# GpSimd adds the four squared tiles of a group, TensorE sums one

## The chip, the cores and the metric

One core of a Trainium2 chip runs the whole program in one launch. The metric is the device time in microseconds, the median of several runs.

## What is computed

Three transformer blocks one behind the other on 512 tokens of 1024 numbers, each a mixer and a gated feed-forward layer with norms and residuals around them. The first mixer is a sparse attention, the second a state-space scan (SSD), the third a short convolution. The change lies in the second, in the norm behind the scan:

```python
y = ssd_scan(x_ssm, dt, a, bm, cm) + d_skip[:, None] * x_ssm
y = y.reshape(b, s, 2048) * silu(z)
yg = y.reshape(b, s, 4, 512)
yg = yg * rsqrt(mean(yg * yg, axis=-1) + eps)      # over the 512 channels of a group
y = (yg.reshape(b, s, 2048) * norm_w) @ w_out
```

The scan goes through the tokens in four chunks of 128 and carries a state from one to the next.

## The kernel before

Everything is kept with channels on the 128 partitions and tokens along the free axis. Each engine has a hand-written program; semaphores order them. Large matrix products run as three passes of TensorE (high and low parts of the weights and of the operand), L664 to L666.

The scan consists of 16 steps, G = 4c + g for chunk c and channel group g; the steps of one chunk work on the four groups. What an engine does in a step is written out in a loop on each of them:

- **TensorE**: `segments(G+1)` (L985, two matmuls of 512 columns), `group_sums(G-2)` (L1030), `outputs(G)` (L1008, and from chunk 1 on L1011, which brings in the state), from G+1 = 4 on `spread_cumsums(G+1)` (L991), then `turn_x(G+2)`, `products_cb(G+2)` and, but for the last chunk, `states(G)` (L1021). At two places a `turn_b` stands before `turn_x`.
- **ScalarE**: `segment_exps(G+1)` (L1394), `terms(G+2)` (L1384, eight short ones), `cumsum_exps(G+1)` (L1402, writes xbuf), `keep_b` at two places (L1409), `group_square(G-1)` (L1418, squares of four tiles of 128 tokens into tmp[:, 1, :], 128x512).
- **VectorE**: `weights(G+1)` (L1954, both operands in SBUF), `gated(G)` (L1964, L1968), `x_dt(G+2)` (L1938), `causal_cb(G+2)` (L1945), `keep_state(G)` (L1980, state times decay, from chunk 1 on; L1983 adds the product).
- **GpSimd**: in its loop over n the decayed copy xdec of group n+1 (L599, chunks 0 to 2), then two multiplications of xbuf for group n+1 (L608, chunks 1 to 3), which `outputs(n+1)` waits for.

There is one buffer for the squares: ScalarE writes those of the next group only when TensorE has summed the last ones (`s_gs`). `group_sums` reads the four tiles as weights against a column of ones, so that the sums come out one token to a partition. The sums of the last group, G = 15, run inside the output product behind the scan (`last_sums`); before it stand the norm's steps for the other groups on VectorE and ScalarE and `spread_group` (L1037). A matmul in float32 leaves two records or more in the trace.

Of the kernel before, what the change touches and what calls it, by code (L numbers as in the profile page):

```python
# [9 lines left out]
ALU = mybir.AluOpType  # L10
# [4 lines left out]
P = 128  # L15
S = 512
NT = S // P
# [196 lines left out]
def build(nc, w8, w22, xT, params, heads, w_cmp, w_ada, out):  # L214
    with ExitStack() as ctx:
        def sem(name):
            return ctx.enter_context(nc.semaphore(name))
# [3 lines left out]
        def sb(name, shape, dt=F32, at=None):  # L221
            size = 4 * int(np.prod(shape[1:]))
            size = (size + 31) // 32 * 32
            if at is None:
                at = base[0]
                base[0] += size
            assert at + size <= 229344, (name, at + size)
            t = nc.alloc_sbuf_tensor_at(name, shape, dt, offset=at)
            where[name] = at
            return t  # L230
# [10 lines left out]
        tmp = sb("tmp", [P, 2, S])  # L241
        ident = sb("ident", [P, P])
        ones = sb("ones", [P, P])
# [86 lines left out]
        stat_ps, bc_ps = bank[5], bank[4]  # L330
# [88 lines left out]
        s_cx = sem("c_scaled")  # L419
        s_y = sem("y_made")  # L420
        s_gq = sem("group_squares_made")
        s_gs = sem("group_sums_made")
        s_gn = sem("group_norm_steps")
        s_gr = sem("group_roots_made")
# [47 lines left out]
        def psum_ap(t):  # L472
            return bank[t][:, :]
# [55 lines left out]
        @block.gpsimd  # L529
        def _(pool):  # L530
            chain = Chain(pool, s_pool)
            chain(pool.memset(ident[:, :], 0.0))
            chain(pool.memset(ones[:, :], 1.0))
            chain(pool.memset(mbig[:, :], 0.0))
            chain(pool.memset(mcmp[:, :, :], 0.0))
            chain(pool.memset(rowok[:, :], 1.0))
            chain(pool.memset(pcmp[:, :, :, :, :], 0.0))
            chain(pool.memset(usum[:, :], 1.0))
            chain(pool.memset(after[:, :], 1.0))
            chain.wait()  # L540
            chain(pool.affine_select(out=usum[:, :], in_=usum[:, :], compare_op=ALU.is_ge, fill=0.0,
                                     base=0, pattern=[[1, P]], channel_multiplier=-1))
            chain(pool.affine_select(out=after[:, :], in_=after[:, :], compare_op=ALU.is_ge, fill=0.0,
                                     base=-1, pattern=[[-1, P]], channel_multiplier=1))
            chain(pool.affine_select(out=ident[:, :], in_=ident[:, :], compare_op=ALU.not_equal, fill=1.0,
                                     base=0, pattern=[[-1, P]], channel_multiplier=1))

            chain(pool.affine_select(out=mbig[:, :], in_=mbig[:, :], compare_op=ALU.is_ge, fill=NEG,
                                     base=S - P, pattern=[[-1, S]], channel_multiplier=1))

            chain(pool.affine_select(out=mcmp[:, :, :], in_=mcmp[:, :, :], compare_op=ALU.is_ge, fill=NEG,
                                     base=-31, pattern=[[P, NT], [-16, NC]], channel_multiplier=1))
            chain(pool.affine_select(out=rowok[:, :], in_=rowok[:, :], compare_op=ALU.is_ge, fill=0.0,
                                     base=-31, pattern=[[0, 1]], channel_multiplier=1))
            chain.wait()
            pool.memset(small[:, 31:32], 0.0).then_inc(s_const, 1)

            def add_update(before):

                for j in range(KD):  # L560
                    pool.wait_ge(s_add, before + j + 1)
                    pool.tensor_tensor(h[:, j, :], tmp[:, j % 2, :], h[:, j, :], ALU.add).then_inc(s_h, 1)  # L562

            def ada(half):

                for s in range(ADA_HALF * half, ADA_HALF * (half + 1)):
                    acc = ada_acc[:, s % 2, :]
                    for k in range(KD):
                        n = KD * s + k
                        w = ada_w[:, n % ADA_RING, :]  # L570
                        pool.wait_ge(s_ada_w[n % ADA_RING], 16 * (n // ADA_RING + 1))
                        if k == 0:
                            if s >= 2:
                                pool.wait_ge(s_adap, s - 1)
                            pool.tensor_scalar(acc, w, csil[:, 0:1], 1.0, ALU.mult, ALU.mult).then_inc(s_ada_k, 1)  # L575
                            continue
                        chain(pool.tensor_scalar(w, w, csil[:, k:k + 1], 1.0, ALU.mult, ALU.mult))  # L577
                        chain.wait()
                        pool.wait_ge(s_ada_k, n)
                        pool.tensor_tensor(acc, acc, w, ALU.add).then_inc(s_ada_k, 1)  # L580

            pool.wait_ge(s_sq, 1)
            pool.memset(vz[:, :, :, :], 0.0).then_inc(s_vz, 1)
            pool.wait_ge(s_csil, 1)
            add_update(0)
            ada(0)
            add_update(KD)
            for n in range(-1, 4 * NT):
                c, g = (n + 1) // 4, (n + 1) % 4
                if c >= NT:  # L590
                    continue
                if c < NT - 1:

                    pool.wait_ge(s_xd, n + 2)
                    pool.wait_ge(s_dec, 1)
                    if c:
                        pool.wait_ge(s_st, n - 2)
                    hs = slice(8 * g, 8 * g + 8)
                    pool.tensor_tensor(xdec[:, hs, :], xdt[:, hs, :],  # L599
                                       acs[:, 1, c, hs].unsqueeze(2).to_broadcast([P, 8, HD]),  # L600
                                       ALU.mult).then_inc(s_xdec, 1)
                if c:
                    tok = slice(c * P, (c + 1) * P)
                    for U in (2 * n + 2, 2 * n + 3):

                        pool.wait_ge(s_xe, U - 8 + 1)
                        b = xbuf[:, U % 4, :].rearrange("p (a l) -> p a l", a=4)
                        pool.tensor_tensor(b, b, cv[:, 4 + g, tok].unsqueeze(1).to_broadcast([P, 4, P]),  # L608
                                           ALU.mult).then_inc(s_cx, 1)
            add_update(2 * KD)  # L610
            ada(1)

# [2 lines left out]
        def _(pe):  # L615
# [44 lines left out]
            def product(bk, g, kb, k, last, hi, lo):  # L660

                w = g % SLOTS
                cols = slice(kb * P, (kb + 1) * P)
                pe.matmul(bk, whi[w][:, cols], hi[:, k, :], start=k == 0, stop=False)  # L664
                pe.matmul(bk, whi[w][:, cols], lo[:, k, :], start=False, stop=False)  # L665
                return pe.matmul(bk, wlo[w][:, cols], hi[:, k, :], start=False, stop=last)  # L666
# [62 lines left out]
            for kb in range(KD):  # L729
                pe.wait_ge(s_xt, XT["NSA_IN"] + kb + 1)  # L730
                for c in range(3):
                    if kb == 0:
                        pe.wait_ge(s_lo, c + 1)
                    mm = product(psum_ap(c), c, kb, kb, kb == KD - 1, xhi, xlo)
# [16 lines left out]
            for c in range(V_FIRST, V_FIRST + 4):  # L751
                pe.wait_ge(s_lo, c + 1)
                w = c % SLOTS
                for kk in range(2):
                    k = 2 * (c - V_FIRST) + kk
                    cols = slice(kk * S, (kk + 1) * S)
                    for t in range(NT):
# [4 lines left out]
                        mm = pe.matmul(bk, xlo[:, k, tk], whi[w][:, cols], start=False, stop=k == KD - 1)  # L762
# [26 lines left out]
            for g in range(4):  # L789
                for hh in range(2):  # L790
                    mm = pe.matmul(bank[4][(g % 2) * HD:(g % 2 + 1) * HD, (g // 2) * NC:(g // 2 + 1) * NC],
                                   w2[0][:, hh, :], hg[:, hh, g, 0:NC], start=hh == 0, stop=hh == 1)
# [5 lines left out]
            for g in range(4):  # L798
                for hh in range(2):
                    mm = pe.matmul(bank[5][:, g * HD:(g + 1) * HD],  # L800
                                   hv[:, hh, g, :, :].rearrange("p q c -> p (q c)"),
                                   w2[1][:, hh, :], start=hh == 0, stop=hh == 1)
            mm.then_inc(s_cm, 1)
            pe.wait_ge(s_gate, 1)
            for t in range(NT):
                mm = pe.transpose(bank[6][:, t * 48:(t + 1) * 48], gt[:, t * P:(t + 1) * P], ident[0:48, 0:48])
# [218 lines left out]
            def group_sums(G):  # L1025

                c, g = G // 4, G % 4
                pe.wait_ge(s_gq, G + 1)
                for r in range(4):
                    mm = pe.matmul(stat_ps[:, 4 * g + c:4 * g + c + 1], tmp[:, 1, r * P:(r + 1) * P], ones[:, 0:1],  # L1030
                                   start=r == 0, stop=r == 3)
                mm.then_inc(s_gs, 1)

            def spread_group(g):

# [14 lines left out]
            for G in range(4 * NT):  # L1050
                c, g = G // 4, G % 4
# [14 lines left out]
                if c < NT - 1:  # L1066
                    states(G)
            group_sums(4 * NT - 2)

            pe.wait_ge(s_gn, 2)  # L1070
# [7 lines left out]
            def last_sums():  # L1078

                group_sums(4 * NT - 1)  # L1080
# [1139 lines left out]
```

## Time and profile before

| | |
|---|---|
| median of three runs | 2267.5 us (2264.09 to 2268.2) |
| the profiled execution, its own time | 2270.14 us |
| its span, first to last instruction | 2268.4 us |
| TensorE busy | 2174.0 us (96%) |
| VectorE, ScalarE, GpSimd busy | 1269.9, 854.4, 289.4 us |
| mean granted clock of TensorE | 0.971 of 2.4 GHz |

Busy time is the sum of an engine's instructions, the span what passes from the first to the last; an engine's share says only how much of the time it works, not whether others wait for it. The scan lies between about 1030 and 1152 us of the span.

### The profile page before, as it was taken

Reading aid. Unit: us, or ns where it says so; the run is one execution under the profiler, and the core shown is the slowest. Engines: PE = TensorE matmul, PEld = TensorE weight load, DVE = VectorE, ACT = ScalarE, POOL = GpSimd, SP = SyncE. Lnnn points to the kernel's source line nnn. Section 1 sums busy time; section 2 is a strip of 40 time slices with the busy share of each in tenths; the row PEclk is TensorE's granted clock in tenths of the full one; section 3 lists DMA queues with packets and bytes.
Section 4 is the critical chain, followed back from the end, with each engine's and each line's share of the span. In section 5 each row is a group of like instructions: output and inputs, shape, how many; then the busy total and the mean of one; then the engine's idle time right before and its main releaser. Section 6 shows DMA issues by size and latency. Waiting matters only on the chain.

```text
span 2268.4 us, 27014 instructions
## 1 busy us (share of the span) xinstructions
PE 2174.0 (96%) x10560; PEld 1728.7 (76%) x10560; DVE 1269.9 (56%) x2112; ACT 854.4 (38%) x1438; POOL 289.4 (13%) x200
## 2 busy tenths in 40 slices
PE   8999989999999999998999999999999999999997
PEld 6876667788888778885678788888778877888885
DVE  4267663777755578636763687764455445333333
ACT  4156662444432254426642444432221223222221
POOL 0000000200029600002400200009700000000000
PEclk9999989999999999999999999999979988999998
DMA  8210002233246423220013132236512212223231
GB/s 260 61 41 29 20 11 65 65 103 95 96 135 199 145 75 111 93 91 22 1 29 102 51 117 93 93 114 197 181 49 91 93 65 75 93 95 98 89 93 54
DMA packets 59790, 203.57 MB, mean 90 GB/s; under 512 B 6800, under 2 KB 7312, under 8 KB 59408
## 3 DMA queue, kind: packets, MB, share of 16 engines
q1 hardware_dynamic: 55920, 191.36, 26.2%
q10 hardware_dynamic: 3744, 10.49, 1.4%
q8 instruction: 84, 1.38, 0.2%
q14 instruction: 42, 0.34, 0.0%
HBM read 197.63 MB, written 2.10 MB: 88 GB/s over the span
## 4 chain that ended last, share of the span: by engine, by line
PE 90%; DVE 5%; ACT 4%; issue 1%; POOL 1%; DMA 0%; SPq 0%; DVEq 0%; ACTq 0%; POOLq 0%
PE bank L664 25%; PE bank L665 25%; PE bank L666 25%; PE bank L619 2%; ACT pbuf L1268 1%; PE bank L985 1%; PE bank L774 1%; PE bank L869 1%; DVE pbuf L1740 1%; PE bank L991 1%; PE bank L823 1%; PE bank L846 1%; PE bank L646 1%; PE bank L1008 1%; ACT pt L1285 1%
## 5 line engine op out<-in xcount | busy, mean ns | idle before, releaser
L664 PE MATMUL bank<-xhi,whi 128*128 128x512 f32 x1712 | 686.6, 401 | 28.9 <-DVE xlo L1515 22.6
L665 PE MATMUL bank<-xlo,whi 128*128 128x512 f32 x1712 | 681.1, 398 | 0.0
L666 PE MATMUL bank<-xhi,wlo 128*128 128x512 f32 x1712 | 680.9, 398 | 0.0
L1125 ACT ACTIVATE whi<-raw 128x1024 fp32r<-128x1024 f32 (+1 forms) x322 | 334.2, 1040 | 773.3 <-PE bank L666 706.1
L1503 DVE TENSOR_TENSOR wlo<-raw,whi 128x1024 fp32r<-128x1024 f32 (+1 forms) x322 | 412.4, 1282 | 367.9 <-ACT whi L1125 367.2
L664 PEld LDWEIGHTS bank<-xhi,whi 128*128 128x128 f32 x1712 | 324.5, 190 | 110.5 <-issue 13.1
L666 PEld LDWEIGHTS bank<-xhi,wlo 128*128 128x128 f32 x1712 | 323.9, 189 | 79.6
L665 PEld LDWEIGHTS bank<-xlo,whi 128*128 128x128 f32 x1712 | 324.6, 190 | 77.1
L664 PE MATMUL bank<-hid_hi,whi 128*128 128x512 f32 x528 | 209.5, 397 | 0.0
L665 PE MATMUL bank<-hid_lo,whi 128*128 128x512 f32 x528 | 208.6, 395 | 0.0
L666 PE MATMUL bank<-hid_hi,wlo 128*128 128x512 f32 x528 | 208.5, 395 | 0.0
L666 PEld LDWEIGHTS bank<-hid_hi,wlo 128*128 128x128 f32 x528 | 99.0, 187 | 24.2
L665 PEld LDWEIGHTS bank<-hid_lo,whi 128*128 128x128 f32 x528 | 99.0, 188 | 23.8
L664 PEld LDWEIGHTS bank<-hid_hi,whi 128*128 128x128 f32 x528 | 99.0, 188 | 23.7
L580 POOL TENSOR_TENSOR ada_acc<-ada_acc,ada_w 128x768 f32<-128x768 f32 x56 | 116.0, 2071 | 4.7
L1619 DVE TENSOR_TENSOR upad<-bank,rstd_b 128x512 f32<-128x512 f32 x88 | 60.6, 690 | 78.0 <-PE bank L666 71.6
L562 POOL TENSOR_TENSOR h<-tmp,h 128x512 f32<-128x512 f32 x24 | 38.0, 1619 | 497.4 <-DVE tmp L1546 497.4
L1183 ACT ACTIVATE tmp<-upad,par 128x512 f32<-128x512 f32 x88 | 70.6, 804 | 27.0 <-DVE upad L1619 27.0
L1268 ACT ACTIVATE pbuf<-pbuf,stat 128x512 f32<-128x512 f32 (+3 forms) x128 | 70.1, 551 | 23.7 <-DVE stat L1743 23.7
L575 POOL TENSOR_SCALAR ada_acc<-ada_w,csil 128x768 f32<-128x768 f32 x8 | 12.2, 1524 | 509.4 <-DMA ada_w<-w_ada 509.4
L577 POOL TENSOR_SCALAR ada_w<-ada_w,csil 128x768 f32<-128x768 f32 x56 | 74.8, 1335 | 0.8 <-DMA ada_w<-w_ada 0.7
L1631 DVE SCALAR_TENSOR_TENSOR tmp<-upad,par,tmp 128x512 f32<-128x512 f32 x88 | 66.2, 752 | 3.1
(271 smaller groups left out, 2540.7 us busy)
## 6 DMA issues: line engine op xcount, KB each, us to landing
raw<-w SPq DMA_DIRECT2D x298, 512.0 KB, 3.6
ada_w<-w_ada SPq DMA_DIRECT2D x64, 384.0 KB, 3.1
raw<-w SPq DMA_DIRECT2D x24, 384.0 KB, 3.4
h<-xT ACTq DMA_DIRECT2D x8, 256.0 KB, 9.4
w_k<-w_cmp ACTq DMA_DIRECT2D x1, 2048.0 KB, 8.5
w_v<-w_cmp ACTq DMA_DIRECT2D x1, 2048.0 KB, 7.8
out_t<-h ACTq DMA_DIRECT2D x8, 256.0 KB, 2.0
dk<-stg ACTq DMA_DIRECT2D x2, 256.0 KB, 6.8
```

The lines of the kernel that those rows point to most:

```text
L577: chain(pool.tensor_scalar(w, w, csil[:, k:k + 1], 1.0, ALU.mult, ALU.mult))
L580: pool.tensor_tensor(acc, acc, w, ALU.add).then_inc(s_ada_k, 1)
L619: mm = pe.matmul(stat_ps[:, t:t + 1], src[:, t * P:(t + 1) * P], ones[:, 0:1], start=first and t == 0, stop=last, skip_group_check=True)
L664: pe.matmul(bk, whi[w][:, cols], hi[:, k, :], start=k == 0, stop=False)
L665: pe.matmul(bk, whi[w][:, cols], lo[:, k, :], start=False, stop=False)
L666: return pe.matmul(bk, wlo[w][:, cols], hi[:, k, :], start=False, stop=last)
L1125: act.activation(whi[g % SLOTS][:, 0:n], raw[g % RAWS][:, 0:n], ACT.Copy).then_inc(s_hi, 1)
L1183: act.activation(tmp[:, c % 2, :], upad[:, c % 2, 2:2 + S], ACT.Identity, scale=col("ffn_w", 3 * k + 2), bias=col("ffn_b", k)).then_inc(s_ ...
L1268: act.activation(pbuf[:, s % 3, g, 0:n], pbuf[:, s % 3, g, 0:n], ACT.Exp, scale=QSCALE, bias=stat[:, b, 4 + g:5 + g], accum_out=stat[:, b, ...
L1503: dve.tensor_tensor(wlo[g % SLOTS][:, 0:n], raw[g % RAWS][:, 0:n], whi[g % SLOTS][:, 0:n].bitcast(F32), ALU.subtract).then_inc(s_lo, 1)
L1619: dve.tensor_tensor(upad[:, c % 2, 2:2 + S], in_bank(c)[:, :], rstd_b[:, :], ALU.mult)\
L1631: ins = dve.scalar_tensor_tensor(out=tmp[:, v, :], in0=upad[:, v, 0:S], scalar=col("ffn_w", 3 * k), in1=tmp[:, v, :], op0=ALU.mult, op1=AL ...
```

## The change

GpSimd gets `add_squares(G)`: it waits for the squares of group G, adds tiles 2 and 3 onto tiles 0 and 1 (128x256), waits for its own result, and adds tile 1 onto tile 0 (128x128). Then it signals `s_ga`. It does so in its loop for group n-1, behind the work for group n+1; the last two groups stand behind the loop. TensorE waits for `s_ga` in the place of `s_gq` and makes one matmul on tile 0 in the place of four. Nothing else is changed; ScalarE's squares still wait for TensorE's sums.

```diff
+        s_ga = sem("group_squares_added")
...
+            def add_squares(G):
+
+                pool.wait_ge(s_gq, G + 1)
+                chain(pool.tensor_tensor(tmp[:, 1, 0:2 * P], tmp[:, 1, 0:2 * P], tmp[:, 1, 2 * P:4 * P], ALU.add))
+                chain.wait()
+                pool.tensor_tensor(tmp[:, 1, 0:P], tmp[:, 1, 0:P], tmp[:, 1, P:2 * P], ALU.add).then_inc(s_ga, 1)
+
             for n in range(-1, 4 * NT):
                 c, g = (n + 1) // 4, (n + 1) % 4
                 if c >= NT:
...
                         pool.tensor_tensor(b, b, cv[:, 4 + g, tok].unsqueeze(1).to_broadcast([P, 4, P]),
                                            ALU.mult).then_inc(s_cx, 1)
+                if n >= 1:
+                    add_squares(n - 1)
+            for G in (4 * NT - 2, 4 * NT - 1):
+                add_squares(G)
             add_update(2 * KD)
...
             def group_sums(G):
 
                 c, g = G // 4, G % 4
-                pe.wait_ge(s_gq, G + 1)
-                for r in range(4):
-                    mm = pe.matmul(stat_ps[:, 4 * g + c:4 * g + c + 1], tmp[:, 1, r * P:(r + 1) * P], ones[:, 0:1],
-                                   start=r == 0, stop=r == 3)
-                mm.then_inc(s_gs, 1)
+                pe.wait_ge(s_ga, G + 1)
+                pe.matmul(stat_ps[:, 4 * g + c:4 * g + c + 1], tmp[:, 1, 0:P], ones[:, 0:1],
+                          start=True, stop=True).then_inc(s_gs, 1)
```

The line numbers of the changed kernel are 8 higher in GpSimd's loop and 12 higher on TensorE. GpSimd's order in chunk 2, before (xdec, xbuf: the multiplications named above; the words in brackets are the semaphores waited for):

```order
L608 TENSOR_TENSOR xbuf<-xbuf,cv 128x512 [waits spread_exps] x2
L599 TENSOR_TENSOR xdec<-xdt,acs 128x512 [waits state_products,decays_made,x_dt_made]
L608 TENSOR_TENSOR xbuf<-xbuf,cv 128x512 [waits spread_exps] x2
L599 TENSOR_TENSOR xdec<-xdt,acs 128x512 [waits state_products,decays_made,x_dt_made]
L608 TENSOR_TENSOR xbuf<-xbuf,cv 128x512 [waits spread_exps] x2
```

and in the changed kernel:

```order
L616 TENSOR_TENSOR xbuf<-xbuf,cv 128x512 [waits spread_exps] x2
L592 TENSOR_TENSOR tmp<-tmp 128x256 [waits group_squares_made]
L594 TENSOR_TENSOR tmp<-tmp 128x128 [waits pool_chain]
L607 TENSOR_TENSOR xdec<-xdt,acs 128x512 [waits state_products,decays_made,x_dt_made]
L616 TENSOR_TENSOR xbuf<-xbuf,cv 128x512 [waits spread_exps] x2
L592 TENSOR_TENSOR tmp<-tmp 128x256 [waits group_squares_made]
L594 TENSOR_TENSOR tmp<-tmp 128x128 [waits pool_chain]
```

The two additions of group n-1 stand directly behind the two xbuf multiplications of group n+1 and ahead of the next xdec.

TensorE's order around the same place, before (the banks and buffers with their numbers; L985 is segments, L1030 the sums, L1008 and L1011 the outputs):

```order
L985 MATMUL bank0<-vbuf2_124,after_121 128x512 [waits spread_exps,segment_terms_made]
L985 MATMUL bank1<-vbuf3_125,after_121 128x512 [waits spread_exps,segment_terms_made]
L1030 MATMUL bank5<-ones_66,tmp_64 128x1 [waits group_squares_made]
L1030 MATMUL bank5<-ones_66,tmp_64 128x1 x3
L1008 MATMUL bank2<-ebuf_119,xdt_114 64x128 [waits c_scaled,ssd_weights_made,state_kept,y_kept,x_dt_made]
```

and in the changed kernel:

```order
L997 MATMUL bank0<-vbuf2_124,after_121 128x512 [waits spread_exps,segment_terms_made]
L997 MATMUL bank1<-vbuf3_125,after_121 128x512 [waits spread_exps,segment_terms_made]
L1041 MATMUL bank5<-ones_66,tmp_64 128x1 [waits group_squares_added]
L1020 MATMUL bank2<-ebuf_119,xdt_114 64x128 [waits c_scaled,ssd_weights_made,state_kept,y_kept,x_dt_made]
```

Three matmuls are gone; the one left stands at the same place, in front of the outputs, and waits for GpSimd in the place of ScalarE.

## Rows read from the trace of the kernel before

**Rows 1.** The page, part 4: shares of the chain that ended last.
```profile
PE 90%; DVE 5%; ACT 4%; issue 1%; POOL 1%; DMA 0%; SPq 0%; DVEq 0%; ACTq 0%; POOLq 0%
```

**Rows 2.** Timeline of step 9: start us, us, engine, line, operation, [idle before <-releaser].
```profile
1090.34 1.98 PE L991 MATMUL bank<-vbuf,ones 128*128 128x512 f32 x4
...
1092.17 2.50 POOL L608 TENSOR_TENSOR xbuf<-xbuf,cv 128x512 f32<-128x512 f32 x2 [5.45 <-ACT xbuf L1402]
...
1092.85 0.62 ACT L1418 ACTIVATE tmp<-zb 128x512 f32<-128x512 f32 x1
...
1093.88 1.34 DVE L1980 TENSOR_TENSOR state<-state,acs 128x512 f32<-128x512 f32 x1 [0.20 <-PE bank L1021]
...
1094.62 1.50 POOL L599 TENSOR_TENSOR xdec<-xdt,acs 128x512 f32<-128x512 f32 x1
...
1095.39 0.95 PE L1030 MATMUL bank<-ones,tmp 128*128 128x1 f32 x8
...
1095.86 1.41 DVE L1954 TENSOR_TENSOR sqr<-sqr,cbuf 128x512 f32<-128x512 f32 x2
...
1096.27 0.45 PE L1008 MATMUL bank<-ebuf,xdt 128*64 128x128 f32 x4
...
1098.22 1.98 PE L991 MATMUL bank<-vbuf,ones 128*128 128x512 f32 x4
```

**Rows 3.** Timeline of step 13, in the last chunk.
```profile
1129.76 1.98 PE L991 MATMUL bank<-vbuf,ones 128*128 128x512 f32 x4
...
1131.60 2.50 POOL L608 TENSOR_TENSOR xbuf<-xbuf,cv 128x512 f32<-128x512 f32 x2 [5.39 <-ACT xbuf L1402]
...
1133.96 0.95 PE L1030 MATMUL bank<-ones,tmp 128*128 128x1 f32 x8
...
1134.00 1.48 DVE L1954 TENSOR_TENSOR ebuf<-ebuf,cbuf 128x512 f32<-128x512 f32 x2 [0.90 <-ACT ebuf L1394]
...
1134.84 0.45 PE L1008 MATMUL bank<-sqr,xdt 128*64 128x128 f32 x4
```

**Rows 4.** Timeline of step 15.
```profile
1143.81 1.98 PE L991 MATMUL bank<-vbuf,ones 128*128 128x512 f32 x4
...
1147.00 1.05 PE L1030 MATMUL bank<-ones,tmp 128*128 128x1 f32 x8 [1.20 <-ACT tmp L1418]
...
1147.98 0.45 PE L1008 MATMUL bank<-sqr,xdt 128*64 128x128 f32 x4
```

**Rows 5.** GpSimd by line: duration ns min/median/max; the last row: busy us, mean ns, idle us before.
```profile
L562 POOL TENSOR_TENSOR h<-tmp,h x24: 1260/1732/1762, 399.3 to 1269.4; 128x512 f32<-128x512 f32 x24
...
L580 POOL TENSOR_TENSOR ada_acc<-ada_acc,ada_w x56: 1817/1854/2702, 668.6 to 1626.6; 128x768 f32<-128x768 f32 x56
...
L599 POOL TENSOR_TENSOR xdec<-xdt,acs x12: 1041/1249/1497, 1037.1 to 1110.4; 128x512 f32<-128x512 f32 x12
...
L580 POOL TENSOR_TENSOR ada_acc<-ada_acc,ada_w 128x768 f32<-128x768 f32 x56 | 116.0, 2071 | 4.7
```

**Rows 6.** Timeline of step 1: VectorE and GpSimd together.
```profile
1039.78 2.14 DVE L1954 TENSOR_TENSOR sqr<-sqr,cbuf 128x512 f32<-128x512 f32 x2
...
1039.93 1.45 POOL L599 TENSOR_TENSOR xdec<-xdt,acs 128x512 f32<-128x512 f32 x1 [1.83 <-DVE xdt L1938]
```

**Rows 7.** Timeline of steps 3 and 7: two places where ScalarE is last.
```profile
1058.57 0.60 ACT L1402 ACTIVATE xbuf<-bank 128x512 f32<-128x512 f32 x1
...
1084.22 0.66 PE L964 MATMUL bank<-ident,cv 128*128 128x128 f32 x4 [0.74 <-ACT btok L1409]
```

**Rows 8.** Waits of TensorE (timeline), and windows: length, busy, granted clock, DMA.
```profile
219.31 1.14 PE L846 MATMUL bank<-ident,pbuf 128*128 128x128 f32 x8 [1.43 <-ACT pt L1285]
...
1165.44 0.50 PE L664 MATMUL bank<-yhi,whi 128*128 128x512 f32 x1 [1.51 <-DVE ylo L2006]
...
1148.00:1150.00 2.00, 2.00 (x34) 1.00 0.00 0
1166.00:1170.00 4.00, 4.00 (x12) 0.57 0.00 0
```


## The prediction

> **What bounds the kernel now.** I read four views: the page's chain of work that ended last, the timeline of one step of the scan, the rows of GpSimd's groups, and the granted clock around TensorE's long waits. The chain says that 90% of the span ends on TensorE [rows 1]. So a TensorE instruction less is worth its time, as long as nothing else becomes the last to arrive. In the scan that has to be looked at step by step.
>
> Take the step G = 9 (chunk 2) [rows 2]. I count from t0, the start of spread_cumsums(9) on TensorE at 1090.34. ScalarE takes the exponential of the first bank, and GpSimd starts scaling xbuf at t0+1.83; its two multiplications take 2.50 us, and its next instruction starts at 1094.62, t0+4.28. Meanwhile ScalarE made the squares of group 7 at 1092.85, well before. TensorE, without a gap, does segments(10), then the sums of group 7 at 1095.39, then outputs(9) at 1096.27, t0+5.93, and spread_cumsums(10) at 1098.22: a period of 7.88 us with no wait of TensorE. The eight records of the sums (two passes for each of four matmuls) hold it from 1095.39 to 1096.27, 0.88 us, 0.11 us each.
>
> In the last chunk a step is shorter, because it has no state product: from t0 = 1129.76 to outputs(13) at 1134.84 is 5.08 us, though GpSimd's two multiplications stand at the same distance from t0 [rows 3]. In the last step, outputs(15) follows t0 = 1143.81 by 4.17 us, after a wait of 1.20 us for the squares [rows 4].
>
> **What the change removes.** Three of four matmuls per group: 6 of 8 records, 6/8 of 0.88 = 0.66 us, and for 16 groups 10.6 us at most.
>
> **What it adds.** On GpSimd two additions a group, 128x256 and 128x128, both from SBUF to SBUF, 32 instructions. The trace has no such shape. Nearest are the two-input instructions of 128x512 (1260 ns at the least) and 128x768 (1817 ns at the least) [rows 5]: 557 ns for 256 columns, 2.18 ns a column, and some 145 ns apart from the columns. That gives 0.70 and 0.42 us. The second waits for the first by a semaphore: behind such a wait the 56 accumulations of 128x768 sat idle 4.7 us in all, 0.08 us each. The pair takes **1.20 us** undisturbed. From below: the fastest 128x512 row, 1041 ns with a broadcast operand, taken by its columns alone, gives 0.78 us for 384 columns. From above: each addition once held up by a VectorE instruction, which comes next. The Trainium skill, "GPSIMD Engine Reference", section 3.1, measures 4497 ns for an addition of 2048 columns; an estimate in proportion is 0.84 us for the pair, and the sum below would be some 3 us smaller by it. The same section says that VectorE should do elementwise work, which speaks against this change.
>
> **VectorE holds GpSimd up.** A VectorE instruction with two operands in SBUF and a GpSimd instruction exclude each other in this trace. VectorE's weights, of the same shape, take some 0.7 us each; its state <- state,acs starts at 1093.88, lasts 1.34, and so ends 1095.22, while GpSimd's multiplication was running until about 1094.6; GpSimd's xdec, started at 1094.62, then takes 1.50 instead of 1.04 us [rows 2, 5]. So xdec really began at t0+4.74. A second case shows who comes next: VectorE started a pair at 1039.78 and GpSimd one at 1039.93, which ended at 1041.38; the pair took 2.14 us instead of some 1.4 [rows 6]. GpSimd got in between the two, 0.56 us behind the start of the first (1041.38 - 1.04 - 1039.78). The Trainium skill, "SBUF — State Buffer", section "Who interferes with whom", has it as a rule: whoever gets the shared ports first keeps them for the whole instruction. By that rule, the trace agrees, additions placed where xdec stands now are held up as xdec is.
>
> **Where the additions stand.** In GpSimd's order add_squares(G-2) comes right behind the two multiplications of group G, so it cannot start before t0+4.28, although its squares are ready at t0+3.1. TensorE must have it for the sums, and outputs(G) is queued behind the sums; behind that, spread_cumsums(G+1), which starts the next period. So the loop spread, exponential, two multiplications, two additions, sums, outputs, spread becomes a closed one through four engines.
>
> - **Steps 5 to 12** (VectorE's state update runs there). First addition 4.74 + 0.70 = 5.44; second from 5.52. VectorE's weights start at 1095.86, also t0+5.52: a tie. If GpSimd wins, it ends at 5.94; if VectorE wins, GpSimd gets in at about 6.08 and ends at 6.50. Add 0.05 us for the semaphore and 0.32 us for the two records of a drained TensorE (the last but one sums took 0.98 us from 1147.00 to 1147.98 for eight; less 0.66) [rows 4]. outputs(G) starts at 6.31 or 6.87 instead of 5.93: +0.38 or +0.94; I take the middle, +0.66. In step 7 TensorE waits for ScalarE's copy of B anyway, so that its period is longer [rows 7], the additions are covered, and the 0.66 us is won. Seven steps: +4.6 (2.7 to 6.6); one: -0.7.
> - **Steps 13 and 14.** VectorE's weights are first in line at t0+4.24 (1134.00) and, having waited for GpSimd's multiplication, start about 0.1 later; GpSimd follows 0.56 behind, at 4.90, and ends the first addition at 5.60. The second half of the weights then takes 0.69 from about 5.5, GpSimd gets in at 6.1 and ends at 6.5; outputs start at 6.9 instead of 5.08. +1.8 each, **+3.6**. Undisturbed it would be 4.28 + 1.20 + 0.37 = 5.85, +0.77.
> - **Step 15.** No weights follow; outputs(15) at t0+5.85 instead of 4.17: **+1.7**.
> - **Steps 2 to 4**: nothing. In step 4 the multiplications wait for ScalarE, which at 1058.57 comes to the exponential without an idle moment [rows 7], so an earlier spread wins nothing.
> - **Last sums**, inside the next matrix product: four matmuls become one, **-0.7**; the addition was done long before.
>
> Together 4.6 - 0.7 + 3.6 + 1.7 - 0.7 = **+8.5 us**.
>
> **The clock.** TensorE's new waits: in steps 13 and 14 from where the sums stand now (1133.96, t0+4.2) to 6.5, 2.3 us; in step 15 from t0+1.98 to 5.5, 3.5 us; in steps 5 to 12 from 5.05 to 5.95 or 6.5, 0.9 to 1.4 us. Of the eight waits of 1.4 to 2.9 us that TensorE has between 200 us and the product behind the scan, six were followed by a fall to 1.2 GHz (the first is that of 1.43 us, the last that of 1.51 us); behind the one of 1.20 us the clock stayed at 1.00 [rows 4, 8]. Behind the last, the clock stood at 0.57 over 4 us: 0.43 of 4 us, 1.7 us lost. Three new long waits, six in eight, 1.7 us: **+3.8**.
>
> **Sum.** +12.3 us on the profiled execution's 2270.1: 2282.4. That execution lies 2.6 above the median of the runs, 2267.5, so the forecast for a median is **2280**.
>
> **Rivals.**
> 1. *The additions are not held up* (0.20). For it: xdec takes 1.04 us at the least and 1.25 in the middle of its twelve rows, so about half were not held up, and the two sides could fall clear of each other once the period shifts. Against: at this very place it was, by 0.46 us [rows 2, 5]. Then outputs start at 5.85: seven steps -0.1 each, step 7 -0.7, steps 13 and 14 +0.8 each, 15 +1.7, last sums -0.7: +1.2, with one fall of the clock +2.9: **2270.5**, inside the noise.
> 2. *Faster: TensorE's saving comes through* (0.06). For it: TensorE bounds the scan, and GpSimd idles 5.4 us before the xbuf multiplications shown [rows 2, 3]. It needs the additions ready where the sums stand now, t0+5.05, that is a pair of at most 0.7 us (5.05 - 4.28 - 0.05) that nothing holds up; the lower bound is 0.78 us. Then steps 5 to 12 and the last sums win 0.66 us each, -5.9; steps 13 and 14 have outputs at 4.28 + 0.7 + 0.37 = 5.35, +0.3 each, and step 15 +1.2: -4.1, **2263**. At a pair of 1.3 us (5.93 - 0.37 - 4.28) nothing is left of the gain in steps 5 to 12.
> 3. *The clock falls in steps 5 to 12 too* (0.12). The waits there, 0.9 to 1.4 us, recur every 8 us. Eight more falls at 1.7 us: +14, **2294**.
>
> The forecast case (held up, clock falling in the last chunk) has 0.62.
>
> **How the numbers follow.** Its own range is 2275 (GpSimd wins every tie, one fall) to 2284 (VectorE wins, three falls). The range takes in rival 1 and most of the way to rival 3: **2269 to 2291**. Differences below 0.2%, 4.5 us, can't be told from no change. Slower than 2272: 0.62, 0.12 and 0.02 of rival 1, less 0.01 where the ties all go one way, 0.75. Faster than 2263: most of rival 2 and what may be missing from both views, 0.05. Within: 0.20.
>
> **What the changed profile would show.** Right: TensorE's sums shrink to 32 records; in front of them a new idle row with GpSimd's second addition as the releaser, 0.7 us or more in steps 5 to 12 and about 2 in 13 and 14; the 128x256 additions at 0.70 us alone and above 1.1 beside VectorE; periods of 8.3 to 8.8 us in chunks 1 and 2 and about 9 in chunk 3; a granted clock below 1.00 between 1130 and 1155. Wrong: additions of 0.5 us, periods of 7.2 us and no idle row; or a clock of 0.5 all through chunks 1 and 2.

## The result, and the profile after

| | before | changed |
|---|---|---|
| median of four runs | 2267.85 us | 2283.03 us |
| lowest to highest | 2264.09 to 2270.28 | 2279.79 to 2285.03 |
| the profiled execution's span | 2268.4 us | 2278.0 us |

The ratio is 1.0067, with an interval of 1.0048 to 1.0086: the changed kernel is slower by 15 us. A second measurement on another occasion gave 2282.5 us and a ratio of 1.0073 (1.0061 to 1.0086). The profiled execution was the fastest of its four, so its span shows less than the medians.

The page of the changed kernel: TensorE has 96 records less and 10 us less of busy time, GpSimd 27 us more; in the chain that ended last (second row) TensorE's share fell from 90% to 87% and GpSimd's rose from 1% to 3% [rows 1]. The freed engine now waits in the chain for the one that got the work.

```profile
PE 2163.6 (95%) x10464; PEld 1715.8 (75%) x10464; DVE 1270.3 (56%) x2112; ACT 854.5 (38%) x1438; POOL 316.1 (14%) x232
...
PE 87%; DVE 5%; ACT 4%; POOL 3%; issue 1%; DMA 0%; SPq 0%; DVEq 0%; POOLq 0%; ACTq 0%
```

One label first. TensorE's first spread is that of group 4, at 1057.40 before the change; counted from there, the spread at 1090.34 is the fifth, that of group 8. So the step of [rows 2], which the prediction calls step 9, is step 8, with the sums of group 6. Its times and sums are not touched by this: steps 8 to 12 all have the same period. (The rows under experiments 1, 3, 4 and 6 are of step 9 itself.) A step G is here what passes from spread_cumsums(G) to the next spread.

The timeline of step 8, which answers to [rows 2] (L1003 is the spread, L616 the multiplications, L1428 the squares, L1990 the state update, L592 and L594 the additions, L1964 the weights, L1041 the sums, L1020 the outputs):

```profile
1089.09 1.98 PE L1003 MATMUL bank<-vbuf,ones 128*128 128x512 f32 x4
...
1090.92 2.49 POOL L616 TENSOR_TENSOR xbuf<-xbuf,cv 128x512 f32<-128x512 f32 x2 [3.50 <-ACT xbuf L1412]
...
1091.60 0.62 ACT L1428 ACTIVATE tmp<-zb 128x512 f32<-128x512 f32 x1
...
1092.63 1.33 DVE L1990 TENSOR_TENSOR state<-state,acs 128x512 f32<-128x512 f32 x1 [0.20 <-PE bank L1033]
...
1093.37 1.17 POOL L592 TENSOR_TENSOR tmp<-tmp 128x256 f32<-128x256 f32 x1
...
1094.60 1.54 DVE L1964 TENSOR_TENSOR sqr<-sqr,cbuf 128x512 f32<-128x512 f32 x2
1094.62 0.97 POOL L594 TENSOR_TENSOR tmp<-tmp 128x128 f32<-128x128 f32 x1
...
1095.65 0.38 PE L1041 MATMUL bank<-ones,tmp 128*128 128x1 f32 x2 [1.34 <-POOL tmp L594]
...
1095.96 0.45 PE L1020 MATMUL bank<-ebuf,xdt 128*64 128x128 f32 x4
...
1097.91 1.98 PE L1003 MATMUL bank<-vbuf,ones 128*128 128x512 f32 x4
```

With t0 = 1089.09 everything up to 1093.37 lies where it lay before: GpSimd's next instruction starts at t0+4.28, which is now the first addition. It takes 1.17 us: VectorE's state update, issued at t0+3.54, ran first when the multiplication ended (experiment 6 takes it away). VectorE's weights and the second addition start almost together, at t0+5.51 and t0+5.53, and the addition takes 0.97 us. TensorE has waited 1.34 us when the sums may start, and outputs(8) begins at t0+6.87 in place of t0+5.93. The next spread is at t0+8.82, not 7.88.

The next rows are the starts of the spread and of the sums on TensorE, in brackets its wait and who ended it, in steps 4 and 5 and from step 13 to the norm behind the scan:

```profile
1054.00 1.98 PE L1003 MATMUL bank<-vbuf,ones 128*128 128x512 f32 x4
...
1060.55 0.38 PE L1041 MATMUL bank<-ones,tmp 128*128 128x1 f32 x2 [1.33 <-POOL tmp L594]
...
1062.81 1.98 PE L1003 MATMUL bank<-vbuf,ones 128*128 128x512 f32 x4
...
1080.48 1.98 PE L1003 MATMUL bank<-vbuf,ones 128*128 128x512 f32 x4
...
1133.23 1.98 PE L1003 MATMUL bank<-vbuf,ones 128*128 128x512 f32 x4
...
1139.66 0.38 PE L1041 MATMUL bank<-ones,tmp 128*128 128x1 f32 x2 [2.07 <-POOL tmp L594]
...
1141.92 1.98 PE L1003 MATMUL bank<-vbuf,ones 128*128 128x512 f32 x4
...
1148.36 0.38 PE L1041 MATMUL bank<-ones,tmp 128*128 128x1 f32 x2 [2.07 <-POOL tmp L594]
...
1151.98 2.22 PE L1003 MATMUL bank<-vbuf,ones 128*128 128x512 f32 x4
1157.80 0.38 PE L1041 MATMUL bank<-ones,tmp 128*128 128x1 f32 x2 [3.60 <-POOL tmp L594]
...
1163.75 5.49 PE L1047 MATMUL bank<-ident,gst 128*128 128x128 f32 x24 [2.45 <-DVE gst L2028]
```

| stretch | before, us | changed, us | difference |
|---|---|---|---|
| step 4, spread to spread | 7.89 | 8.81 | +0.9 |
| steps 5, 6 and 8 to 12, each | 7.88 | 8.83 | +0.95, seven times +6.6 |
| step 7 | 9.28 | 8.61 | -0.7 |
| step 13 | 7.03 | 8.69 | +1.7 |
| step 14 | 7.02 | 10.06 | +3.0 |
| step 15 to the norm (L1037, now L1047) | 9.16 | 11.77 | +2.6 |

That is +14.2 us from the spread of step 4 to the norm. In the profile of the second measurement the same stretch is longer by 2.2 us: 16.4 above the kernel before. Ahead of it, from the scan's first segments (1031.58 before, 1029.34 now) to that spread, 25.8 became 24.7 us; behind it, from the norm to the end, 1115.4 became 1114.3 us.

Step 13 answers to [rows 3]. VectorE's weights were first, the addition got in between their two halves, and the second addition behind the second half:

```profile
1137.47 1.82 DVE L1964 TENSOR_TENSOR ebuf<-ebuf,cbuf 128x512 f32<-128x512 f32 x2 [0.90 <-ACT ebuf L1404]
1137.53 1.22 POOL L592 TENSOR_TENSOR tmp<-tmp 128x256 f32<-128x256 f32 x1
...
1138.83 0.78 POOL L594 TENSOR_TENSOR tmp<-tmp 128x128 f32<-128x128 f32 x1
```

The two kinds of addition over all 16 groups (minimum, median and maximum in ns, of 128x256 and of 128x128):

```profile
L592 POOL TENSOR_TENSOR tmp<-tmp x16: 716/1173/1222, 1045.1 to 1163.4; 128x256 f32<-128x256 f32 x16
```

```profile
L594 POOL TENSOR_TENSOR tmp<-tmp x16: 452/820/975, 1046.2 to 1164.2; 128x128 f32<-128x128 f32 x16
```

And TensorE's clock in the last chunk (length, busy time, granted clock, DMA):

```profile
1130.00:1140.00 10.00, 6.96 (x52) 1.00 0.00 0
1140.00:1148.00 8.00, 6.29 (x47) 1.00 0.01 2
1148.00:1150.00 2.00, 1.64 (x18) 0.77 0.00 0
1150.00:1152.00 2.00, 2.00 (x21) 0.50 0.00 0
1152.00:1154.00 2.00, 2.00 (x5) 0.88 0.00 0
1159.00:1161.00 2.00, 2.00 (x23) 0.58 0.00 0
```

It answers to [rows 8]: 1.00 through the waits of steps 12 and 13 (and in all of 1046 to 1130), then 0.50 behind the 2.07 us wait of step 14, and 0.58 behind the 3.60 us of step 15.

### The profile page after: what moved, and what is told of

Its sections match the earlier page's. It is cut to its first block, busy times and chain, and to the rows that moved or that the text cites. A ratio compares the mean times of both kernels' runs of the same rounds, so it can differ in the third digit from the quotient of the medians.

```text
span 2278.0 us, 26854 instructions
## 1 busy us (share of the span) xinstructions
PE 2163.6 (95%) x10464; PEld 1715.8 (75%) x10464; DVE 1270.3 (56%) x2112; ACT 854.5 (38%) x1438; POOL 316.1 (14%) x232
## 3 DMA queue, kind: packets, MB, share of 16 engines
q8 instruction: 83, 1.36, 0.2%
## 4 chain that ended last, share of the span: by engine, by line
PE 87%; DVE 5%; ACT 4%; POOL 3%; issue 1%; DMA 0%; SPq 0%; DVEq 0%; POOLq 0%; ACTq 0%
PE bank L676 25%; PE bank L677 25%; PE bank L678 25%; PE bank L631 2%; ACT pbuf L1278 2%; DVE pbuf L1750 1%; PE bank L786 1%; POOL xbuf L616 1%; PE bank L881 1%; PE bank L835 1%; PE bank L858 1%; PE bank L658 1%; PE bank L1020 1%; POOL h L563 1%; ACT pt L1295 1%
```

## The experiments

All were timed against the kernel before on the same chip. t0 is always the start of the spread.

**1. The sums one place later.**

```diff
-                if G >= 2:
-                    if G == 2:
-                        pe.wait_ge(s_acv, 1)
-                    group_sums(G - 2)
                 outputs(G)
+                if G >= 2:
+                    if G == 2:
+                        pe.wait_ge(s_acv, 1)
+                    group_sums(G - 2)
```

> The changed kernel with one thing moved: on TensorE the sums of group G-2 stand behind outputs(G) in place of in front of it. Nothing is left out. If the cost is the closed loop (multiplications, additions, sums, outputs, spread), the additions, ready some 6.5 us after t0, are covered by the outputs, which then end about 7.2 us after t0; every wait of 1.3 to 3.6 us before the sums goes, the steps win 0.66 us each, and the time is about 2260 us, 7 us under the kernel before. If the cost is GpSimd's additions themselves, by holding up VectorE wherever the sums stand, it stays near 2283 us.

Measured: 2261.73 us, ratio 0.9971 (0.9959 to 0.9982). The additions are the same, the 15 us are gone, and 6 us of gain stand in their place (7 were expected). A second measurement, for its timeline:

> The kernel with the sums behind the outputs, once more, for its timeline: 2259 to 2263 us. By the closed loop outputs(9) starts 5.2 to 5.3 us after t0, GpSimd's additions still take 1.2 and 1.0 us beside VectorE, and no wait stands before the sums but in step 15.

Measured: 2261.05 us, ratio 0.9973 (0.9964 to 0.9983).

```profile
1096.78 1.96 PE L1003 MATMUL bank<-vbuf,ones 128*128 128x512 f32 x4
...
1098.60 2.50 POOL L616 TENSOR_TENSOR xbuf<-xbuf,cv 128x512 f32<-128x512 f32 x2 [1.19 <-ACT xbuf L1412]
...
1101.05 1.18 POOL L592 TENSOR_TENSOR tmp<-tmp 128x256 f32<-128x256 f32 x1
...
1101.91 0.45 PE L1020 MATMUL bank<-sqr,xdt 128*64 128x128 f32 x4
...
1102.31 0.97 POOL L594 TENSOR_TENSOR tmp<-tmp 128x128 f32<-128x128 f32 x1
...
1103.86 0.38 PE L1041 MATMUL bank<-ones,tmp 128*128 128x1 f32 x2
...
1104.10 1.96 PE L1003 MATMUL bank<-vbuf,ones 128*128 128x512 f32 x4
```

The second addition still ends at t0+6.5, but outputs(G) no longer waits for it: it starts at t0+5.13, and the sums find their tile ready, with no idle time in brackets. The period is 7.32 us, 0.56 less than in the kernel before. No wait stands before the sums of any step. What is left is in step 15: 1.38 us before the outputs, for GpSimd's multiplication, and behind them 2.62 us before the last but one sums, on which only the norm waits.

**2. The same move in the kernel before.**

> The kernel before with the same move: its four matmuls of group G-2 stand behind outputs(G). Nothing is left out. It tells whether the move alone is worth something. The kernel before waits for the sums only in step 15, and there the path ends on the norm's first step, which comes out at the same time by either order; so both theories expect 2266 to 2269 us, no change.

Measured: 2268.13 us, ratio 1.0005 (0.9996 to 1.0014). The move by itself wins nothing. So experiment 1's gain is the change's own saving, which the closed loop had hidden.

**3. The signal without the additions.**

```diff
-                chain(pool.tensor_tensor(tmp[:, 1, 0:2 * P], tmp[:, 1, 0:2 * P], tmp[:, 1, 2 * P:4 * P], ALU.add))
-                chain.wait()
-                pool.tensor_tensor(tmp[:, 1, 0:P], tmp[:, 1, 0:P], tmp[:, 1, P:2 * P], ALU.add).then_inc(s_ga, 1)
+                pool.memset(small[:, 24:25], 0.0).then_inc(s_ga, 1)
```

> The changed kernel without the additions: GpSimd clears one column of a small tile at their place and signals. It leaves out the adding, so that TensorE sums only the first of the four squared tiles. The queue order and all waits stay. If the length of the additions is what costs, the signal comes 4.4 us after t0, outputs start at 4.8 to 5.3, and the time is about 2261 us. If the place behind the two multiplications, or the signal through a fourth engine, is enough, steps 5 to 12 still wait and the time stays above 2270 us.

Measured: 2261.06 us, ratio 0.9968 (0.9956 to 0.9980).

```profile
1094.96 1.98 PE L1001 MATMUL bank<-vbuf,ones 128*128 128x512 f32 x4
...
1099.23 0.10 POOL L592 MEMSET small<- 128x1 f32 x1
...
1100.02 0.28 PE L1039 MATMUL bank<-ones,tmp 128*128 128x1 f32 x2
...
1102.17 1.98 PE L1001 MATMUL bank<-vbuf,ones 128*128 128x512 f32 x4
```

The signal comes at t0+4.4, the sums start at t0+5.06 behind the segments with no wait, the period is 7.21 us. The place in GpSimd's queue and the handover through it cost nothing in chunks 1 and 2, nor in steps 13 and 14, which show no wait before the sums either; the length of the additions does. In step 15 alone the place has a price: TensorE waits 2.43 us for the signal there, where the kernel before waited 1.20 us for the squares.

**4. One addition.**

```diff
-                chain(pool.tensor_tensor(tmp[:, 1, 0:2 * P], ...))
-                chain.wait()
-                pool.tensor_tensor(tmp[:, 1, 0:P], ...).then_inc(s_ga, 1)
+                pool.tensor_tensor(tmp[:, 1, 0:2 * P], tmp[:, 1, 0:2 * P], tmp[:, 1, 2 * P:4 * P],
+                                   ALU.add).then_inc(s_ga, 1)
...
-                pe.matmul(... tmp[:, 1, 0:P] ...)
+                for r in range(2):
+                    mm = pe.matmul(... tmp[:, 1, r * P:(r + 1) * P] ..., start=r == 0, stop=r == 1)
```

> The changed kernel with the first addition alone (128x256); TensorE sums two tiles in place of one. Nothing is left out. By the closed loop outputs start 5.45 + 0.05 + 0.54 = 6.04 us after t0, 0.1 later than before in steps 5 to 12, 1.0 in steps 13 and 14, 1.4 in step 15, less 0.44 in step 7 and in the last sums: +3.3 us, with one fall of the clock +5: 2271 to 2273 us. If the cost went by the count of groups, whatever the additions take, it would be near the 2283 us of the changed kernel.

Measured: 2272.07 us, ratio 1.0019 (1.0010 to 1.0028).

```profile
1101.35 1.18 POOL L592 TENSOR_TENSOR tmp<-tmp 128x256 f32<-128x256 f32 x1
...
1102.58 0.61 PE L1041 MATMUL bank<-ones,tmp 128*128 128x1 f32 x4 [0.30 <-POOL tmp L592]
```

The addition ends at 1102.53, and TensorE waits 0.30 us in place of 1.34. The period is 8.00 us (the sums start at 1102.58 and again at 1110.58), 0.12 above the kernel before. So half the work on each side comes out nearly even in chunks 1 and 2, as the sum of the loop's parts says.

**5. Additions for the first eleven groups alone.** In the sums `if G > 10` takes the old wait and the four matmuls, and GpSimd's loop adds for `1 <= n <= 11` only.

> The changed kernel, with GpSimd's additions for groups 0 to 10 alone; the sums of groups 11 to 15 (steps 13 to 15, the last but one and those in the output product) are four matmuls behind ScalarE's squares, as before. Nothing is left out. By the closed loop and its clock what is left is steps 5 to 12: +0.94 in seven, -0.66 in step 7, about +5.9 us: 2273 to 2274 us, with no fall of the clock in chunk 3. If the last three steps cost nothing of their own, it stays at 2283 us; if the waits in steps 5 to 12 are covered, it falls to 2267 us.

Measured: 2274.16 us, ratio 1.0040 (1.0027 to 1.0054), beside 2282.5 for the changed kernel. Some 7 us belong to steps 4 to 12, some 8 to steps 13 to 15 and what follows. In its timeline TensorE waits 1.34 to 1.36 us before the sums of steps 8 to 12, as in the changed kernel, and 1.21 us in step 15, as before the change.

**6. The instruction that holds the first addition up.**

```diff
-                    chain(dve.tensor_tensor(state[:, hs, :], state[:, hs, :],
-                                            acs[:, 2, c, hs].unsqueeze(2).to_broadcast([P, 8, HD]), ALU.mult))
-                    chain.wait()
                     dve.tensor_tensor(state[:, hs, :], state[:, hs, :], pr, ALU.add).then_inc(s_stk, 1)
```

> The changed kernel without VectorE's product of the state with its decay (the state is summed undecayed, so the outputs differ). It takes away the instruction that holds up the first addition. By the ports the first addition takes 0.72 us in steps 5 to 12 in place of 1.17 and ends at t0+5.0; the second meets VectorE's weights in a tie, so that outputs start at 5.9 to 6.4 in place of 6.87: 3 to 7 us off the changed kernel, 2276 to 2280 us. If the additions are long of themselves, they stay at 1.17 and 0.97 us, and the time at 2283 us.

Measured: 2279.11 us, ratio 1.0053 (1.0040 to 1.0066); its runs (2275.03 to 2280.57) lie wholly under those of the changed kernel beside it (2281.23 to 2283.82).

```profile
1095.04 1.98 PE L1003 MATMUL bank<-vbuf,ones 128*128 128x512 f32 x4
...
1099.33 0.74 POOL L592 TENSOR_TENSOR tmp<-tmp 128x256 f32<-128x256 f32 x1
...
1100.14 1.55 DVE L1964 TENSOR_TENSOR ebuf<-ebuf,cbuf 128x512 f32<-128x512 f32 x2 [0.87 <-ACT ebuf L1404]
1100.14 1.00 POOL L594 TENSOR_TENSOR tmp<-tmp 128x128 f32<-128x128 f32 x1
...
1101.51 0.45 PE L1020 MATMUL bank<-sqr,xdt 128*64 128x128 f32 x4
...
1103.46 1.98 PE L1003 MATMUL bank<-vbuf,ones 128*128 128x512 f32 x4
```

The first addition starts at t0+4.29 as ever and takes 0.74 us in place of 1.17. The second, now 0.4 us earlier, starts in the same hundredth as VectorE's weights (L1964), which were earlier too, and takes 1.00 us. outputs(G) starts at t0+6.47 in place of 6.87, the period is 8.42 us: the outputs come a little later than the 6.4 us that I had expected at most. Seven steps shorter by 0.41 us are 2.9 us, and the medians differ by 3.4.

**7. The waits filled.**

```diff
+                    if G >= 13:
+                        for r in range(3 if G < 15 else 6):
+                            pe.matmul(bank[5][:, 256:384], ones[:, :], ident[:, :], start=True, stop=True)
                     group_sums(G - 2)
```

> The changed kernel with spare matmuls of 128 columns in front of the sums of steps 13, 14 (three each, 1.3 us) and 15 (six, 2.6 us), into unused columns. Nothing is left out. They lie in waits of 2.1 and 3.6 us and lengthen nothing. If the clock's falls in the last chunk are part of the cost, it stays at 1.00 from 1130 to 1160 us, outputs take 1.95 us in each step, and the time is 2 to 4 us under the changed kernel. If the falls cost nothing, the times are equal.

> The changed kernel itself, beside the other three on the same chip: 2280 to 2285 us.

Measured: 2278.95 us (2278.72 to 2280.67), ratio 1.0059 (1.0046 to 1.0072), against 2282.5 us (2281.23 to 2283.82), ratio 1.0073. The intervals of the ratios overlap, the runs do not, and the mean granted clock was 0.972 in all five runs with filled waits, 0.969 in all five of the changed kernel. The same stretch of both, first the kernel with filled waits, then the changed kernel, with the 4 us behind its waits of steps 13 and 14:

```profile
1134.00:1160.00 26.00, 20.81 (x162) 0.99 0.00 1
```

```profile
1134.00:1160.00 26.00, 18.26 (x104) 0.87 0.00 1
1140.00:1144.00 4.00, 4.00 (x35) 0.59 0.01 4
1150.00:1154.00 4.00, 3.87 (x35) 0.57 0.00 0
```

In this execution of the changed kernel both waits of 2.07 us were followed by half the clock; in the one shown above only the second was, and so it was in the profile of experiment 6. The spare matmuls keep the clock at 0.99 up to step 15, and TensorE's remaining wait before the sums there is 1.40 us in steps 13 and 14. They did not keep the clock up in step 15, where 2.27 us of waiting were left and the clock was 0.67 from 1160 to 1164.

**8. One place later still.** The sums stand behind `spread_cumsums(G + 1)`.

> The changed kernel with the sums behind spread_cumsums(G+1), one place later still, so that nothing of the loop is queued behind them. Nothing is left out. If the sums behind the outputs are covered already, it is the same, 2260 to 2263 us. If they hold up the spread there, even by their own 0.22 us a step, it is some 2 us faster.

Measured: 2260.46 us, ratio 0.9972 (0.9963 to 0.9982). Its period is 7.27 us (1099.56 to 1106.83), 0.05 under that of experiment 1; the times cannot be told apart. Both beat the kernel before by 0.3%, and the changed kernel by 1%.

## Why the prediction was right

**The direction and its cause.** The forecast was that the additions enter a loop through four engines, in front of the outputs. Experiments 1 and 3 show both halves: the same additions off the loop cost nothing, and the loop without their length costs nothing but a longer wait in step 15. GpSimd's work as such, and its hold on VectorE, is no cost here: in experiment 1 it is all there.

**Steps 5 to 12.** I took the middle of a tie at t0+5.52, +0.66; VectorE went first in every step, and outputs start at 6.87, the very upper value. Seven steps cost 6.6 us in place of 4.6. Undisturbed, the additions took 0.72 and 0.45 us; I had 0.70 and 0.42, from the slope between two longer rows. Experiment 6 shows the reason of the rest for the first addition: without VectorE's state update it takes 0.74 us in place of 1.17. For the second, no run takes the weights away; its 0.97 us beside them, against 0.45 in step 15, where no weights run, is the evidence. Step 7 won 0.7 us as computed.

**Steps 2 to 4.** Here a step failed: "nothing". Step 4 costs 0.9 us. I had only asked whether an earlier spread would help, and not placed the additions: VectorE does not yet multiply the state by its decay there, so the first takes 0.72 us, but the second (0.79 us) has to take turns with the weights, whose pair takes 1.95 us, and outputs(4) starts at t0+6.87. It is the same loop. What saved part of the sum is that the stretch ahead of step 4 is 1.2 us shorter. Of this, 0.7 us lie between segments(4) and the first spread, which start 3.62 us apart before and 2.95 us after the change: the matmuls taken away, in a step for which I had forecast nothing. The other 0.5 us lie ahead of segments(1), before any sums, where TensorE does the same in both kernels; the granted clock over the ten microseconds around the scan's start was 0.66 in the execution before and 0.83 in the changed one, so they are no gain of the change.

**Steps 13 and 14.** +1.8 each was forecast, the first gave +1.7, by the order that I had written down: weights, addition, weights, addition. Step 15 gave outputs at t0+6.13 in place of 5.85: the additions did not start at 4.28 but at 4.51, since the half clock had stretched the spread. From the outputs to the norm it then took 5.64 us in place of 4.99, with the clock at half in part of it; the whole step cost +2.6 in place of +1.7.

**The clock.** +3.8 was forecast, from three waits and six falls in eight. (I had left a ninth wait out of the count, that of 1.98 us before the norm at 1152.97; the clock behind it was 0.60 over 4 us, so it is seven in nine, and the term hardly moves.) Step 14 shows it best: +3.0 us, of which 1.7 are step 13's loop and 1.3 the clock. In the profile two of three waits were followed by half the clock, in the second measurement's profile the one of step 13 as well, and that step took 10.29 us in place of 8.69. Filling part of all three waits took 3.5 us off the median.

**The sum.** The signs are right, but the sum came out near in part by luck, since errors went both ways. Against the 12.3 us forecast, the profiled execution has +2.0 in steps 5 to 12, +0.9 in step 4, -1.2 ahead of it, -1.8 in steps 13 to 15 with the clock counted in (7.3 us, where 5.3 and 3.8 for the clock were forecast) and -0.5 behind the norm (-1.2, where -0.7 was in the sum). That leaves 11.8 us from the scan's start to the end. Its span shows only 9.6 us, because some 2 us were lost on the way to the scan in the execution before, where the two kernels are the same.

The medians differ by 15.2 us. The profiled execution was the fastest of its four, with a mean clock of 0.972, and the other three had 0.969, as had the second measurement, whose profile has three falls. For VectorE first everywhere and three falls, the terms of the prediction give 8.5 + 2.0 + 5.1 = 15.6 us, 2283.1 for the median, against 2283.03 measured; step 3 and step 4, which it leaves out, nearly cancel with -0.7 and +0.9. (The ends of its own range, 2275 and 2284, are 2275.8 and 2283.1 by the same terms.) So what was undersized is the middle taken for the tie and the number of falls. Rival 1, additions not held up, fell with the 1.17 and 0.97 us; rival 2 with the waits; rival 3 did not occur, as the waits of 1.34 us left the clock at 1.00.

## What to carry to other kernels

Work handed from a busy engine to an idle one was not free here, because what waited for its result was queued in front of the critical work. Ask at once for the place of the consumer in its own queue: here the result was needed by nobody for a whole step, and moving one matmul by one place turned +0.7% into -0.3%. And price the new work at the time of the step in which it will run, with the instruction of VectorE that runs there, not by its length alone.

## What I had not expected of the hardware

How closely the second addition and VectorE's weights met. In the changed kernel, in steps 5, 6 and 8 to 12, VectorE's weights started first each time, but by no more than 0.03 us, and the 128x128 addition took 0.97 us, with 0.45 us undisturbed. The weights' pair grew too, from 1.41 to 1.54 us in step 8, since its second half then waited for the addition. In experiment 6, where everything before had moved by 0.4 us, the two met again, though it was now ScalarE's exponential that released the weights and no longer the state update: both start within 0.01 us of each other in seven steps, the addition once ahead by that much, and it took 0.99 to 1.01 us in all of them. Whether VectorE wins a true tie, or was first by less than the trace resolves, no run here tells.
